# Output projection of a hybrid residual block: from 32 weight units times four token blocks to seven block products, 56 half-size units

## What is computed

```python
h = rmsnorm(x, mix_pre_g);  proj = h @ w_in                  # conv input, pool input, gates
y_a = silu(layernorm(causal_conv(glu(proj)))) @ w_a_out      # branch A
y_b = (per-group map of trailing means) @ w_b_out            # branch B
merged = g_a * y_a + g_b * y_b                               # sigmoid gates
x = x + rmsnorm(merged @ w_o, mix_post_g)                    # <- the output projection
h2 = rmsnorm(x, ffn_pre_g)
x = x + rmsnorm((gelu(conv3(h2 @ w_gate)) * conv3(h2 @ w_val)) @ w_down, ffn_post_g)
x = x + rmsnorm((p @ w_ple) * sigmoid(x @ w_ple_gate), ple_post_g)
```

## Time and profile before

| | us |
|---|---|
| device time, three runs | 2549.11, 2552.56, 2554.24 (median 2552.56) |
| span of the profiled execution, first to last instruction | 2549.2 |
| PE busy in the span | 2512.1 (99%) |
| DVE busy | 1839.5 (72%) |
| ACT busy | 1021.6 (40%) |
| output projection on PE, first to last matmul start | 811.8 to 985.8 |

### The profile page before, as it was taken

One profiled execution on the slowest core, in us unless ns is written; L12 is line 12 of the kernel. 1 busy time (PEld: TensorE's weight loads), 2 busy tenths in 40 slices (PEclk: granted clock), 3 DMA queues, 4 the chain that ended last, 5 costly groups with the idle time before them and its releaser, 6 DMA issues. The chain is left out here.

```text
span 2549.2 us, 36122 instructions
## 1 busy us (share of the span) xinstructions
PE 2512.1 (99%) x14276; PEld 2207.3 (87%) x14276; DVE 1839.5 (72%) x2226; ACT 1021.6 (40%) x1199; POOL 184.7 (7%) x261
## 2 busy tenths in 40 slices
PE   9999999999999999999999999999999999999998
PEld 7788888888888888899999999999987878877886
DVE  7888766653334236889899998999988787888434
ACT  5222322252223224444444444444454453455323
...
GB/s 170 104 103 91 105 94 99 91 116 96 94 99 108 149 98 128 157 178 221 207 189 215 207 220 200 197 217 204 219 272 243 256 245 190 270 235 227 89 98 68
DMA packets 153554, 418.71 MB, mean 164 GB/s; under 512 B 12992, under 2 KB 46784, under 8 KB 152384
## 3 DMA queue, kind: packets, MB, share of 16 engines
...
HBM read 379.66 MB, written 36.96 MB: 163 GB/s over the span
## 5 line engine op out<-in xcount | busy, mean ns | idle before, releaser
L1082 ACT ACTIVATE w_hi<-ring_raw 128x1024 fp32r<-128x1024 f32 x426 | 450.3, 1060 | 603.1 <-PE ps L980 389.7
L1504 DVE TENSOR_TENSOR ring_lo<-ring_raw,w_hi 128x1024 fp32r<-128x1024 f32 x426 | 518.3, 1221 | 189.8 <-ACT w_hi L1082 188.4
L1493 DVE TENSOR_TENSOR w_lo<-w_raw,w_hi 128x1024 fp32r<-128x1024 f32 x192 | 234.4, 1224 | 405.2 <-ACT w_hi L1072 404.9
L1072 ACT ACTIVATE w_hi<-w_raw 128x1024 fp32r<-128x1024 f32 x192 | 202.6, 1059 | 515.4 <-PE ps L760 366.0
L758 PE MATMUL ps<-xg_hi,w_hi 128*128 128x512 f32 x1024 | 400.7, 391 | 4.9 <-DVE w_lo L1493 3.3
L759 PE MATMUL ps<-xg_lo,w_hi 128*128 128x512 f32 x1024 | 399.1, 390 | 0.0
L760 PE MATMUL ps<-xg_hi,w_lo 128*128 128x512 f32 x1024 | 399.0, 390 | 0.0
L978 PE MATMUL ps<-s_hi,w_hi 128*128 128x256 f32 x1280 | 361.4, 282 | 2.5 <-issue 2.4
L980 PE MATMUL ps<-s_hi,ring_lo 128*128 128x256 f32 x1280 | 361.7, 283 | 0.0
L979 PE MATMUL ps<-s_lo,w_hi 128*128 128x256 f32 x1280 | 361.2, 282 | 0.0
L978 PE MATMUL ps<-xg_hi,w_hi 128*128 128x256 f32 x960 | 271.0, 282 | 2.3 <-DVE ring_lo L1504 2.3
...
## 6 DMA issues: line engine op xcount, KB each, us to landing
ring_raw<-in_w_up SPq DMA_DIRECT2D x200, 512.0 KB, 4.9
ring_raw<-in_w_down SPq DMA_DIRECT2D x114, 512.0 KB, 5.1
w_raw<-in_w_in SPq DMA_DIRECT2D x110, 512.0 KB, 3.3
ring_raw<-in_w_up POOLq DMA_DIRECT2D x80, 512.0 KB, 6.3
w_raw<-in_w_o SPq DMA_DIRECT2D x32, 512.0 KB, 3.6
ring_raw<-in_w_ple_gate SPq DMA_DIRECT2D x32, 512.0 KB, 3.6
...
```

The source lines that it names most:

```text
L1082: f(w_hi[:, (U_S + n) % SLOTS], raw_of(n), ACT.Copy).then_inc(hi_ready, 1)
L1493: dve.tensor_tensor(w_lo[:, s], w_raw[:, u.slot(RAW)], as_f32(w_hi[:, s]), ALU.subtract).then_inc(lo_ready, 1)
L1504: dve.tensor_tensor(low_of_unit(n), raw_of(n), as_f32(w_hi[:, (U_S + n) % SLOTS]), ALU.subtract).then_inc(lo_ready, 1)
```

## The change

The product is cut into blocks: tokens into two halves of 256 ("near" and "far"), the 2048 input channels into two halves of eight chunks, and the columns, for each half h of them (1024 columns), into two groups of 512. The four input blocks times four weight blocks are then made by seven block products instead of eight: each has 8 chunks, 2 token blocks and 512 columns, which are four units of 12 matmuls. Two halves h of seven products of four units are 56 units and 672 matmuls. The names of the products are `W11`, `W22`, `T1`, `T2`, `T3`, `T4`, `W21`. Their weight tiles are one block of `w_o` (W11, W22, W21) or a sum: T3 and, in the first half, T1 get their second block by a transfer that adds; T2, T4 and, in the second half, T1 are summed by DVE. Their activations are blocks of `merged` or sums of them: the far half of the first eight chunks is replaced by far minus near (`far_differences`, inside the fourth last branch), and three more sums are made at the start of the projection (`out_sum_2`, `out_sum_1`, `out_sum_3`; 2048 numbers per partition each) and split into high and low like the rest. The results are taken out of PSUM by ACT (one copy per W11 product, and one of the W11 + W21 sum in the first half) and folded by DVE (`out_second`, `out_first`, `out_third`, `out_fourth`, `out_other`); W21 adds onto the bank of W11.

In the first half W11, T3 and W21 run one after another, then T1, T2 and T4 unit by unit in turn, then W22. In the second half W11, T1, T2 and T4 take turns, four sums open in all eight banks, and T3, W22 and W21 follow. The raw weight tiles get a ring of eight buffers, in which the low part replaces the raw one. The residual x is loaded at the end of T2 of the second half, behind unit 42 (counted from 0). Token blocks 2 and 3 are finished first, then block 0 and block 1; PE transposes in that order, with five small matmuls on constants (`keep_clock(5)`) behind the first pair, which stood ahead of the transposes before. Several buffers trade places (`x2`, `og`, `x3` among them).

```diff
+def out_units(h):
+    between = [(mat, q) for q in range(4) for mat in ((T1, T2, T4) if h == 0 else (W11, T1, T2, T4))]
+    before, behind = ((W11, T3, W21), (W22,)) if h == 0 else ((), (T3, W22, W21))
+    return [(mat, q) for mat in before for q in range(4)] + between + [(mat, q) for mat in behind for q in range(4)]
+OUT = [(h, mat, q) for h in range(2) for mat, q in out_units(h)]
+OUT_BANK = ({W11: 0, T3: 1, W21: 0, T1: 2, T2: 3, T4: 0, W22: 3}, {W11: 1, T1: 2, T2: 0, T4: 3, T3: 0, W22: 2, W21: 1})
+OUT_FREE = ({W11: None, T3: None, W21: None, T1: None, T2: None, T4: None, W22: 1},
+            {W11: 4, T1: 2, T2: 5, T4: 6, T3: 7, W22: 8, W21: None})
...
+            for j, (h, mat, q) in enumerate(OUT):
...
+                else:
+                    sp.wait_ge(units_done, U_O + j - O_RING + 1)
+                k, n = 2 * q + (HC if mat in (W21, W22, T2, T3, T4) else 0), 2 * h + (0 if mat in (W11, W21, T4) else 1)
+                sp.dma_start(out_raw[j % O_RING].rearrange("p (k n) -> p k n", n=W),
+                             wo[:, k:k + 2, n * W:(n + 1) * W]).then_inc(out_in[j % O_RING], 16)
...
+            for j, (h, mat, q) in enumerate(OUT):
+                if j == out_last(0, T3):
+                    pool.wait_ge(merged_ready, DC)
+                    pool.dma_start(gain_o[:], on_all(mix_post_g)).then_inc(gain_o_in, 16)
+                if out_adds(j):
+                    k, n = 2 * q, 2 * h + (0 if mat == T1 else 1)
+                    pool.wait_ge(out_in[j % O_RING], out_landed(j))
+                    pool.dma_start(out_raw[j % O_RING].rearrange("p (k n) -> p k n", n=W),
+                                   w_o.rearrange("(k p) n -> p k n", p=P)[:, k:k + 2, n * W:(n + 1) * W],
+                                   accum_op=ALU.add).then_inc(out_added[j % O_RING], 16)
...
+                        for blocks, ready in (((2, 3), 2), ((0,), 2 * NG + 1), ((1,), 2 * NG + 2)):
+                            pe.wait_ge(x2_ready, ready)
                             for c in range(4):
                                 for b in blocks:
                                     mm = pe.transpose(ps[:, turn_bank + c, b * P:(b + 1) * P], src[:, 0, b, c * P:(c + 1) * P], ident[:])
-                                if b == BLK - 1:
+                                if b == 1:
                                     mm.then_inc(turned, 1)
+                            if b == 3:
+                                keep_clock(5)
...
-            for n in range(NG):
-                rows(At(U_O + 8 * n), At(T_O + 4 * n), 4 * ((n + 1) % 2), xg_hi, xg_lo, DC,
-                     wait=(merged_split, 0) if n == 0 else None, by_block=2 if n == NG - 1 else 0)
...
+            def out_ready(j):
+                h, mat, q = OUT[j]
+                if q == 0 and OUT_FREE[h][mat]:
+                    pe.wait_ge(out_taken, OUT_FREE[h][mat])
...
+                if h == 0 and mat in split_at and q == 0:
+                    pe.wait_ge(m_split, split_at[mat])
+                if q == 0 and mat == W21:
+                    pe.wait_ge(out_copied, 1 if h == 0 else 3)
+                if q == 0 and h == 0 and mat == T4:
+                    pe.wait_ge(out_copied, 2)
+                pe.wait_ge(lo_ready, U_O + j + 1)
...
+            for b in range(2):
+                for j in (O_UNITS - 2, O_UNITS - 1):
+                    if b == 0:
+                        out_ready(j)
+                    for kk in range(2):
+                        mm = out_products(j, kk, b)
+                    if b == 1:
+                        mm.then_inc(units_done, 1)
+                    elif j == O_UNITS - 1:
+                        mm.then_inc(blocks_done, 1)
...
+            pe.wait_ge(out_taken, 12)
+            first_pair(U_F, x2, DC, lambda n: pe.wait_ge(x2_ready, 2 * NG + 2 * n + 2), 0, 4)
...
+            late_high(slice(0, TOKH))
+            for j in range(O_UNITS - 2):
+                step(At(U_O + j))
+                if j == 0:
+                    m_high(T2, 1)
+                if j == 1:
+                    m_high(T1, 2)
+                if j == 3:
+                    late_high(slice(TOKH, TOK))
+                    act.wait_ge(m_ready, 2)
+                    out_copy(0, W11, 3)
+                if j == 6:
+                    m_high(W22, 3)
                     load_table(ACT.Sqrt)
...
+                if j == out_last(1, T2):
+                    for n in range(NG):
+                        act.dma_start(x2[:, n], rows_of(x)[:, n]).then_inc(x_back, 16)
+                if j == out_last(1, T3) + 1:
+                    act.wait_ge(out_taken, 11)
+                    out_squares(8, 12)
+                if j == out_last(1, T3) + 3:
+                    act.wait_ge(row_sums_ready, 1)
+                    standard_deviation(D, row_sum[:, 2:BLK], slice(2, BLK))
+                if j == out_last(1, W22):
+                    act.wait_ge(out_taken, 12)
+                    out_squares(12, 14)
+            for b in range(2):
+                if b == 0:
+                    act.wait_ge(blocks_done, 1)
+                else:
+                    act.wait_ge(units_done, U_F)
+                tile_squares(ps[:, 2 * OUT_BANK[1][W21] + b], b, 2, Q_O + 14 + b)
+                act.wait_ge(row_sums_ready, 2 + b)
+                standard_deviation(D, row_sum[:, b:b + 1], slice(b, b + 1))
...
+            def out_split(j):
+                raw = out_raw[j % O_RING]
+                if OUT[j][:2] == (1, W11):
+                    dve.wait_ge(out_in[j % O_RING], out_landed(j))
+                    for i in range(j + 1, j + 4):
+                        dve.wait_ge(out_in[i % O_RING], out_landed(i))
+                        if i > j + 1:
+                            dve.wait_ge(out_sum_ready, out_sums_made(i - 1))
+                        dve.tensor_tensor(out_raw[i % O_RING][:], out_raw[i % O_RING][:], out_raw[(i - 1) % O_RING][:],
+                                          ALU.add).then_inc(out_sum_ready, 1)
...
+                dve.wait_ge(hi_ready, U_O + j + 1)
+                dve.tensor_tensor(out_lo[j % O_RING][:], raw[:], as_f32(w_hi[:, (U_O + j) % SLOTS]), ALU.subtract).then_inc(lo_ready, 1)
...
+            def out_second(h):
+                dve.wait_ge(out_copied, 1 + 2 * h)
+                dve.wait_ge(units_done, U_O + out_last(h, T2) + 1)
+                dve.tensor_tensor(og_part(h, 2), out_ps(h, T2), og_part(h, 3), ALU.subtract).then_inc(out_taken, 1)
...
+            for j in range(O_UNITS - 2):
+                step(At(U_O + j))
+                if j == 0:
+                    out_sum_2()
+                if j == 1:
+                    out_sum_1()
+                if j == 2:
+                    late_low(near, 1)
+                if j == 4:
+                    m_low(T1, 3)
+                if j == 5:
+                    out_sum_3()
+                if j == 6:
+                    m_low(T2, 2)
+                if j == 7:
+                    late_low(far, 4)
+                if j == 9:
+                    m_low(W22, 5)
+                if j == out_last(0, T2):
+                    out_second(0)
+                    out_first(0)
+                if j == out_last(0, T4):
+                    out_third(0)
+                    out_fourth(0)
+                if j == out_last(0, W22):
+                    out_other(0)
+                if j == O_UNITS // 2 + 3:
+                    dve.wait_ge(gain_o_in, 16)
+                if O_UNITS // 2 + 3 <= j < O_UNITS // 2 + 11:
+                    with_gain_o(j - O_UNITS // 2 - 3)
+                if j == out_last(1, T2):
+                    out_second(1)
+                    out_first(1)
+                if j == out_last(1, T3):
+                    out_third(1)
+                    out_fourth(1)
+                if j == out_last(1, T3) + 1:
+                    with_gain_o(8)
+                    with_gain_o(9)
+                if j == out_last(1, T3) + 2:
+                    with_gain_o(10)
+                    with_gain_o(11)
+                    sum_groups(Q_O + 12, slice(2, BLK))
+                if j == out_last(1, W22):
+                    out_other(1)
+                    token_factors(3, slice(2, BLK))
+                    dve.wait_ge(x_back, 16 * NG)
+                    dve.wait_ge(tiles_taken, T_O + 12)
+                    for b in range(2, BLK):
+                        x2_rows(0, b)
+                if j == out_last(1, W22) + 1:
+                    for n in range(1, NG):
+                        x2_rows(n, 2)
+                if j == out_last(1, W22) + 2:
+                    for n in range(1, NG):
+                        x2_rows(n, 3)
+                    with_gain_o(12)
+                    with_gain_o(13)
+            for b in range(2):
+                sum_groups(Q_O + 15 + b, slice(b, b + 1))
+                with_gain_o(14 + b)
+                token_factors(4 + b, slice(b, b + 1))
+                dve.wait_ge(tiles_taken, T_O + 15 + b)
+                x2_rows(0, b)
```

(10 more changed lines are left out.)

275 lines of the change are left out of this document (191 added, 84 removed).

## The result

Device time, eight runs of each kernel on the same chip: before 2552.19 us median (2549.11 to 2554.24), after 2559.14 (2558.67 to 2560.74). The ratio is 1.003, with an interval of 1.002 to 1.004. The forecast was 2551.8 and "no change"; the time lies in the range of 2543 to 2561, on its slow side. Timed again beside the later experiments, the changed kernel gave 2561.77 (ratio 1.0037, 1.0023 to 1.0050).

What follows compares the result with a forecast made beforehand. PE, busy 99% of the span, bounds the kernel. Fewer matmuls -21.8, start +11.3, banks +2.6, tail +6.3, rows -0.5, clock +1.3 sum to -0.8 us: 2552.56 becomes 2551.8, range 2543 to 2561 (8 in 10).

Steps and rivals of the forecast that it cites:

- Start: Projection's start: PE waits at units 5, 6, 7, 11 and 12 for DVE's low parts, together 11.3 us.
- Bank of unit 24: Unit 24 (W22) waits 0.9 to 1.0 us for the bank T2 leaves, its fold being behind unit 26's low part.
- Bank of unit 44: Unit 44 (T3, second half) waits 1.6 us for T2's fold, behind the low part of unit 46's added weight.
- slower rival: Adding transfers land late, at unit 46's weight and T1's in the first half: +8.4 us, 2561.0; chance 0.24.
- second place: T1's weight in the first half: with 6 us load and 12 us add, unit 21 waits 2.7 us.
- Load of x: Residual load moved behind unit 42, beside weight loads; costed at nothing, as eight buffers give cover.
- Tail: Projection's end: DVE's backlog behind unit 47 delays the last residual row to 987.1, costing 6.3 us.
- Clock: PE's clock falls to half once, in the idle time of the tail: 1.3 us lost.
- the -0.5 of the two rows: Before `w_up`'s second transposes PE waits for two residual rows instead of four: 0.5 us gained.
- clock rival: Clock falls more often, behind waits at units 6 and 12 and in the tail: 2554.4; chance 0.10.
- the 6.3 us of one row: Time from an add's issue in the w_up stage, used for unit 46's adding transfer.
- the 8.1 of another: Time of the adds in the w_down stage, 8.1 us, cited for late adding transfers.

Runs made afterwards that it cites:

- e_clock: Changed kernel with small matmuls on constants in PE's waits ahead of units 5, 6 and 12; 2558.20 us, ratio 1.0025 to the kernel before.
- e_noadd2: Changed kernel without the adding transfers of units 44 and 45, which multiply by one block instead of a sum; 2553.38 us, ratio 1.0009 to the kernel before.
- e_fold: Changed kernel with the second half's fold of T2 ahead of unit 46's low part on DVE; 2557.01 us, ratio 1.0021 to the kernel before.
- e_all: Changed kernel with the edits of e_fold, e_start and e_tail together; 2543.02 us, ratio 0.9965 to the kernel before.
- e_sf: Changed kernel with the edits of e_start and e_fold, without that of e_tail; 2545.31 us, ratio 0.9978 to the kernel before.
- e_noadd4: Changed kernel without the adding transfers of units 44 to 47, so T3 multiplies by one block there; 2552.32 us, ratio 1.0001 to the kernel before.
- e_start: Changed kernel with activation sums and splits reordered in DVE's and ACT's lists at the projection's start; 2552.18 us, ratio 1.0002 to the kernel before.
- a_again: The changed kernel itself, unaltered, timed again beside the later experiments; 2561.77 us, ratio 1.0037 to the kernel before.
- e_tail: Changed kernel with three residual rows and two gains moved behind the last residual row ahead of `w_up`; 2558.81 us, ratio 1.0027 to the kernel before.

## Why the prediction was wrong

The mechanism was right; terms of the sum were mis-sized, one of them badly.

- **Start, +11.3: right**, 11.4 measured. Of the places, units 5, 6 and 12 waited 2.2, 3.5 and 2.4 us (forecast 2.4, 3.6, 3.0); units 7 and 11 did not wait in this execution because the clock fell behind unit 6 and PE took 2.5 us longer over the same 12 matmuls. In e_clock, at full clock, units 7 and 11 waited 0.5 and 1.2.
- **Bank of unit 24, 0.9 to 1.0: right**, 1.0.
- **Bank of unit 44: the step that failed.** "I take 11.5, near the first: 11.5 + 3.7 - 13.6 = 1.6 us". Load and add took 17.6 us (8.6 each, and the hand-overs), and 17.6 + 3.7 - 13.6 = 7.7 is the 7.6 measured: formula right, input wrong. I had taken the load from rows without adds beside it and the add from a stage where I did not check how far apart the adds were issued. e_noadd2 shows both inputs right for a quiet queue (4.0 and 6.8) and wrong in the place where they were used. The slower rival had nearly the right size for this place (8.1), and the waits on adding transfers that it named appeared on ACT. Its size was partly luck: it took 6 us for the load and 12 for the add. Its second place, unit 21, did not wait in the changed kernel, where T1's adds are 10 to 13 us apart and take 5.9 to 6.8. The prediction cites the Trainium skill, "DMA: Bandwidth & Descriptors", section "Queues, rings and completion order", that a DMA engine takes turns between its queues. I applied that to the load of x, and did not ask what the adds do to the weight loads beside them, which took 8.8 us with the adds and 3.8 without. Whether taking turns is the reason, no run here shows.
- **Load of x, 0: right for the changed kernel, for a reason that was not in the sum.** It was issued at 949.73, and the first residual row at 983.00 followed the reciprocal (982.81) without a wait. But I costed only the transfers and not their issuing, which takes 3.3 to 6.2 us of ACT's list in the profiles of the changed kernel and its variants (2.3 before). The wait at unit 44 covered it; in e_fold, e_all and e_sf it costs 1.6 to 1.8 us at unit 47, as far as the times of landing and issue show.
- **Tail, +6.3: too high**, 4.3 measured. The gap from PE's last matmul to the first product of `w_up` is 9.7 us in the changed kernel, e_fold, e_noadd4, e_noadd2, e_clock, e_start, a_again and e_sf alike, although PE ended anywhere from 971 to 988. So the backlog is tied to PE's progress, which fits the end of unit 47, as assumed; from there to the last residual row it took 995.97 - 966.80 = 29.2 us, not 30.8.
- **Clock, +1.3: too low.** I counted one fall in the tail. In the changed kernel it fell behind units 6, 12, 44 and in the tail; the one at 12 cost 1.6 (8 matmuls) and the one at 44, behind a wait that I had not seen, 2.4 (12 matmuls). The 1.3 itself was read from a stretch that I called half clock and whose row says 1.00; only the spacing of its matmuls speaks for half. The fall in the tail held about 11 of the first 12 products of `w_up` at 0.43 us each, which is some 2.2 us. The second transposes came 5.15 us behind the first product (at 1003.30) instead of 3.3, so this fall and the -0.5 of the two rows together made +1.85, not +0.8. That the clock rival's "all of these gaps count" does not hold either, the last section shows.

Over all, +6.0 at unit 44, +2.4 behind it, +1.6 at unit 12 and -2.0 in the tail make 8.0 of the 9.2 us between forecast and measurement in the stretch; the rest is the other terms and a pace of up to 0.232 instead of 0.2267 us in some units, whose cause I did not test. The slower rival, which had the wait at unit 44 right to 0.5 us, had got a chance of 0.24: I had let the 6.3 us of one row outweigh the 8.1 of another without asking which of them had the spacing of this place.

## What to carry to other kernels

A transfer's time holds for the spacing in which it was measured. When a change issues adds and loads closer together, take the worst rows of the trace (here 8.1 for an add, 10.2 for a load), not the nearest ones, for whatever stands behind them. And in a list that one engine works off in order, put what frees a bank ahead of what waits for a transfer, and work that waits for another engine behind work that is ready: the order of eight pieces and of one fold was worth 13.8 us (e_sf against the changed kernel, by the medians), where the 96 matmuls less are 21.8. Issuing a transfer is work in the list of its engine as well: ask what stands behind it.

## What the runs showed beside that

A half clock behind a wait is not the same from run to run. a_again waited 2.9 us ahead of unit 12 and stayed at full clock, where the first profile, after 2.2 us, had eight slow matmuls; with small matmuls in the wait it never fell at the start. Where it fell in the projection, some 6 to 14 matmuls of 512 columns in a row took 0.427 instead of 0.227 us each. Where PE had a chain of waits ahead anyway, that cost nothing.

Two places behind the change, PE's first waits for low parts in the ring of `w_up` (L1088: 0.7 to 4.0 us) and at `w_down` (L1134, longest: 1.9 to 5.0 us), differ by 3 us between the profiles of these kernels. From the list of waits from 1090 to 1960 us (us in total, times, longest), the changed kernel and e_tail:

```profile
PE ps L1134 <- DVE ring_lo L1701: 5.5, 4, 2.3
PE ps L1088 <- DVE ring_lo L1701: 2.9, 1, 2.9
```

```profile
PE ps L1134 <- DVE ring_lo L1701: 7.0, 4, 4.7
PE ps L1088 <- DVE ring_lo L1701: 4.0, 1, 4.0
```

In these two profiles the waits take back 2.6 us (7.0 + 4.0 - 5.5 - 2.9), which is as much as e_tail gained in its stretch. And behind the longer waits the clock fell, where it had stayed up in the changed kernel. The changed kernel and e_tail, columns as in the earlier trace rows:

```profile
1110.00:1120.00 10.00, 7.15 (x61) 6.98 (x60) 4.43 (x7) 4.24 (x5) 0.68 (x1) 1.00 1.02 282
1910.00:1920.00 10.00, 6.48 (x28) 4.75 (x27) 9.06 (x9) 8.16 (x7) 3.75 (x5) 1.00 1.04 315
```

```profile
1110.00:1120.00 10.00, 6.05 (x39) 5.87 (x38) 6.05 (x9) 4.33 (x6) 0.00 (x0) 0.83 0.82 220
1910.00:1920.00 10.00, 5.27 (x19) 3.93 (x18) 5.61 (x5) 4.84 (x4) 2.35 (x3) 0.75 1.04 307
```

Waits and clock together are of the size of the 5.4 us that the part behind the first product of `w_up` took longer in e_tail (1564.0 for 1558.7). An edit of 2 to 3 us is therefore better judged by its stretch of the profile beside the time. What sets these two waits was not tested. When PE arrives does not order them: e_all, where it came earliest, took 1557.8 us behind the first product, and e_sf, 3 us later, 1562.0.
